# Where a split weight panel begins in its buffer: 256 bytes from its tokens in every product, in place of 0 or 32 bytes

## The reference, cut to what matters

```python
h = modulate(rms_norm(x_lat, g_attn[l]), sh1, sc1)
gl, mq, mk, mv, nq, nk, nv = mixer_proj(h, w_in, g_qa, w_uq, g_kva, w_ukv, ...)
y_mla = blocked_attention(mq, mk, mv)
y_na = neighborhood_attention(nq, nk, nv, nk_c, nv_c, rpb[l])
x_lat = x_lat + gt1 * gated_merge(gl, y_mla, y_na, w_mla_o[l], w_na_o[l], w_out[l])
...
h2 = modulate(rms_norm(x_lat, g_mlp[l]), sh2, sc2)
x_lat = x_lat + gt2 * jnp.square(jax.nn.relu(h2 @ w_ff1[l])) @ w_ff2[l]
```

## The kernel before, in words

| split matmuls | distance, stationary minus moving | how many |
|---|---|---|
| 512 columns | 0 | 4302 |
| 256 columns | -32 | 5028 |
| 256 columns (`first_features`, context part of k = 0) | 0 | 36 |
| 272 columns (`mv` panel 0) | -32, -96, -160, ... and so on in steps of 64 with k, eight values | 96 |

## Time and profile before

### The profile page before, as it was taken

How to read it: one execution, slowest core, us unless ns; L and a number is a source line. 1 busy time by engine, 2 the same in 40 slices (tenths; PEclk the granted TensorE clock), 3 DMA queues, 4 the chain that set the end, 5 groups by cost and what they waited for, 6 DMA issues and landing times. The chain is left out here.

```text
span 1984.6 us, 30374 instructions
## 1 busy us (share of the span) xinstructions
PE 1945.9 (98%) x12204; PEld 1635.7 (82%) x12204; DVE 1304.4 (66%) x2407; ACT 904.9 (46%) x1635; POOL 52.1 (3%) x78
## 2 busy tenths in 40 slices
PE   7999999999999999999999999999999999999998
PEld 5788778889888888898789899998887788888867
DVE  5447678857886665657665777675666464555886
ACT  4446763325423232456664654443444432234675
POOL 0000000001000000100000000000000000001000
PEclk9999999999999999999999999999999999999999
DMA  7322006543545454433139455554311133432411
GB/s 311 117 95 86 17 28 239 189 158 108 191 175 207 182 196 174 181 133 108 52 127 338 173 188 174 192 188 159 112 61 54 47 123 128 149 127 85 149 44 43
DMA packets 53579, 278.32 MB, mean 140 GB/s; under 512 B 4536, under 2 KB 19128, under 8 KB 24512
## 3 DMA queue, kind: packets, MB, share of 16 engines
q1 hardware_dynamic: 47168, 265.50, 37.2%
q10 hardware_dynamic: 6128, 10.03, 1.6%
q0 software_dynamic: 144, 0.85, 0.1%
HBM read 274.26 MB, written 2.11 MB: 139 GB/s over the span
## 5 line engine op out<-in xcount | busy, mean ns | idle before, releaser
L640 PE MATMUL ps<-t 128*128 128x512 f32 (+1 forms) x1936 | 665.7, 344 | 4.3 <-DVE t L2026 4.3
L641 PE MATMUL ps<-t 128*128 128x512 f32 (+1 forms) x1936 | 658.9, 340 | 0.0
L642 PE MATMUL ps<-t 128*128 128x512 f32 (+1 forms) x1936 | 658.7, 340 | 0.0
L2026 DVE TENSOR_TENSOR t<-t 128x1024 fp32r<-128x1024 f32 (+2 forms) x370 | 414.3, 1160 | 154.2 <-ACT t L1384 153.3
L1384 ACT ACTIVATE t<-t 128x1024 fp32r<-128x1024 f32 (+3 forms) x376 | 358.3, 1001 | 193.9 <-PE ps L642 142.1
L640 PEld LDWEIGHTS ps<-t 128*128 128x128 f32 x1936 | 363.6, 188 | 55.1 <-DVE t L2026 6.6
L642 PEld LDWEIGHTS ps<-t 128*128 128x128 f32 x1936 | 363.6, 188 | 42.5
L641 PEld LDWEIGHTS ps<-t 128*128 128x128 f32 x1936 | 363.7, 188 | 41.8 <-issue 0.7
L2012 DVE TENSOR_TENSOR t<-t 128x256 f32<-128x256 f32 (+9 forms) x622 | 227.1, 386 | 137.9 <-ACT t L1756 38.1
L2021 DVE SCALAR_TENSOR_TENSOR t<-t 128x256 f32<-128x256 f32 (+4 forms) x372 | 273.0, 766 | 36.4 <-ACT t L1489 21.8
L1489 ACT ACTIVATE t<-ps 128x512 f32<-128x512 f32 (+2 forms) x239 | 113.2, 494 | 284.6 <-PE ps L642 188.0
(11 more groups left out here) (191 smaller groups left out, 2314.0 us busy)
## 6 DMA issues: line engine op xcount, KB each, us to landing
t<-in_panels SPq DMA_DIRECT2D x231, 1024.0 KB, 4.9
t<-in_panels SPq DMA_DIRECT2D x12, 768.0 KB, 4.5
t<-in_panels SPq DMA_DIRECT2D x16, 512.0 KB, 3.6
t<-in_window ACTq DMA_DIRECT2D x4, 768.0 KB, 4.3
t<-gates_between ACTq DMA_DIRECT2D x4, 512.0 KB, 4.9
t<-in_panels SPq DMA_DIRECT2D x1, 1088.0 KB, 5.0
t<-in_ctxT SPq DMA_DIRECT2D x1, 1024.0 KB, 6.6
t<-in_xT SPq DMA_DIRECT2D x1, 1024.0 KB, 8.9
```

The lines of the kernel that those rows point to most:

```text
L640: e.matmul(o, hi[:, k, w], xh[:, c0:c1], start=k == 0, stop=False)
L641: e.matmul(o, hi[:, k, w], xl[:, c0:c1], start=False, stop=False)
L642: t = e.matmul(o, lo[:, k, w], xh[:, c0:c1], start=False, stop=k == p.nk - 1)
L2026: e.tensor_tensor(p.half(p.split(wlo), a), p.half(raw[p.slot], a), p.half(p.split(whi), a).bitcast(F32), ALU.subtract).then_inc(*up(ve, (" ...
```

## The change

`first_column` is replaced by a rule of two values. Nothing else changes: the instructions, their order, waits, sizes and DMAs are the same, and only the start addresses of panels within `whi` and `wlo` move.

```diff
 def first_column(key):
-    kind, l, n = key[0], key[1], key[-1]
-    if kind in ("uq", "mv") or kind == "na" and n >= 4:
-        return 8
-    if (kind == "ukv" or kind in ("mo", "no") and len(key) == 3 and l == 0 or kind == "wo" and l == 0 and n < 3
-            or kind == "ff2" and l == 0 and n < 15 or kind == "mw" and n < 7):
-        return 8
-    if kind in ("cq", "ckv", "gm", "gn", "ff1") and l == 1 or kind == "ff1" and n < 2 or kind == "mq" and n < 2 or kind == "atz":
-        return 120
-    return 0
+    kind = key[0]
+    return 72 if kind in ("ukv", "no", "wo", "ff2", "mw", "atw") or kind == "mo" and len(key) == 3 else 64
```

## The result

The changed kernel takes **1994.97 us** (median of 4 executions, 1994.24 to 1995.65), the kernel before 1985.93 in its 4 executions beside it: a ratio of 1.0044, 95% interval 1.0032 to 1.0056. The change costs 9 us. The profiled execution of the changed kernel took 1995.35 us, its span is 1993.2 against 1984.6.

A forecast was written before the change was run, and what follows sets the result against it. TensorE's start-to-start matmul pace was taken as the bound (busy 98% of the span). 512 columns 0, 256 columns +17.1 us, 2 us of waits given back: +15 us, forecast 2001 us, range 1942 to 2025.

The forecast's parts named there:

- the likeliest case: Whole kernel: 512-column matmuls unchanged, 256-column ones slower, 2001 us, its own range 1993 to 2009; chance 0.40.
- reading 3: Eight 256-column matmuls at distance 0, from 19.46 to 20.42 us: 120.0 ns start to start.
- the third rival: Place doesn't matter beyond +-32 near 0, the 3.4 ns belonged to the first 20 us: 1986 us; chance 0.17.
- The rival that 256 is quiet for both sizes: 512- and 256-column matmuls both lose disturbance at distance 256: 1924 us in full, 1955 by half; chance 0.33.
- the bounds: 512-column matmuls up to 34 us slower; undisturbed paces of 220 and 110 ns would gain 29 and 33 us.
- 0 and 256 are alike: Matmuls at distance 256 behave as at 0, since both agree by the remainder of 64: 512 columns stay at 226.7 ns.
- within 0.01 of 0.375: Three 272-column matmuls in the changed kernel were to take within 0.01 of 0.375 us.
- -32 and +32 are alike: Distances of either sign disturb matmuls equally, from the same 8 ns at 512-column panel changes.
- Reading 4: 512-column matmuls at +32 and -32, once each at a panel change: records of 397 and 396 ns against 389.
- 116.6 becomes 120.0, 3.4 ns x 5028: 256-column matmuls going from distance -32 to 256, each 3.4 ns slower: 17.1 us in all.
- Given back: I take half, 2 us: Line 640's waits for VectorE in layer 1, 4.2 us, shrink as TensorE slows: half, 2 us, given back.
- layer 1 longer by some 11 us: Layer 1's window from 830 to 1320 us lengthens by some 11 us, layer 0 and the mLSTM output unmoved.

The follow-up runs named there:

- e3_wide256: Kernel before with distance 256 for the 512-column products alone, the others as before: 1986.48 us against 1987.01, ratio 0.9998.
- e4_narrow256: Kernel before with distance 256 for the 256-column products alone, the others as before: 1995.85 us, ratio 1.0044.
- e7_wide32: Kernel before with distance 32 in place of 0 for the 512-column products, the others as before: 2009.52 us against 1987.55, ratio 1.0114.
- e1_sweep32: Kernel before with successive panels taking sixteen distances in turn, 0 to 480 bytes in steps of 32, counted apart for 512 and 256 columns: 2007.18 us.
- e6: Kernel before with distance 64 for the 256-column products, 0 for the 512-column ones: 1983.21 us against 1987.55, ratio 0.998.
- e8: Kernel before with distance 88 for the 256-column products, 0 for the 512-column ones: 1986.36 us against 1986.99, ratio 0.9999.
- e9: Kernel before with distance 76 for the 256-column products, 0 for the 512-column ones: 1986.9 us, ratio 1.0001.
- e11: Kernel before with 256-column products at 88 bytes where weights are stationary, 64 where tokens are, 512-column ones at 0: 1980.61 us against 1986.77, ratio 0.9971.
- e12: Kernel before with 256-column products at 64 bytes where weights are stationary, 88 where tokens are, 512-column ones at 0: 1986.06 us, ratio 0.9997.

## Why the prediction was right, and where its steps failed

**Direction and place: right.** 2001 was said, 1995 measured: slower, by 9 us instead of 15, within the likeliest case's own range. The losing matmuls are the 256-column ones at 120.0 ns start to start, the 512-column ones stayed at 227, and e3_wide256 and e4_narrow256 show the two halves separately. The 120 of reading 3 was no matter of the first 20 us, as the third rival had it: it holds in layer 1 from 926 us on. VectorE's and ScalarE's busy times are the same. The rival that 256 is quiet for both sizes is refuted: nothing fell. Nor did any of the 47 distances bring the 220 and 110 ns that the bounds took as free of disturbance; the lowest settled means are 226.7 and 113.3. The rule it was weighed against, that the Trainium skill ("TensorE: Matmul & The Clock Gate", part 2, step 1) gives the moving operand and the weight load independent read ports that do not slow each other, does not hold for these matmuls: e7_wide32 moves nothing but start addresses and costs 6.0 ns on each matmul of 512 columns.

**"0 and 256 are alike": right for the wrong reason.** The step that failed is "the coarse place in the 512 bytes counts little and the fine place, by 64, counts". It was drawn from the 272-column matmuls, eight distances with one remainder by 64 and one pace of 125. In e1_sweep32 the distances 0, 64, 128 and 192 give 226.7, 233.4, 232.8 and 228.9, so places that agree by 64 do not agree; those that agree by 256 do. The changed kernel's own 272-column rows show that the eight readings misled: at 0, -256 and +-128 they take 127.1 to 127.6 ns, at +-64 and +-192 124.7 to 125.2, where one value was expected for all. The mean, 125.8, hid it: "within 0.01 of 0.375" came true (3.02 / 8 = 0.378) and proved nothing. Had the change been to 64 or 192, the same reasoning would have said no change from 0 for 512 columns, and lost some 28 us (6.6 x 4302) or 9 (2.2 x 4302).

**"-32 and +32 are alike": roughly.** By 256, -32 is 224. For 512 columns 32 and 224 both give 233.3. For 256 columns they are 118.3 and 117.4, and before's own mean at -32 was 116.85, so even that differs with what stands around it. Reading 4 was thinner than it had to be: the trace of before has not two but thirteen such panel changes among the 512-column products, and each has a record of 396 or 397 ns.

**"116.6 becomes 120.0, 3.4 ns x 5028": 17.1 us said, 14.8 measured.** The rows read were settled ones of one stretch. Over all 256-column intervals without a wait it is 116.85 to 119.84, 3.0 ns, and some 100 of the 256-column intervals hold a wait in one of the two traces and do not count. The likeliest case's bracket has a slip: with the 2 us given back, 1993 to 2009 is 1.9 to 5.1 ns for each 256-column matmul, not 1.7 to 4.7; the 3.0 measured is in either.

**"Given back: I take half, 2 us": the term that was mis-sized.** Waits gave back 4.8 us in the trace (6.2 with the half-clock stretch) and 6 in e4_narrow256. The step looked at one line in one window. In the changed kernel that line's wait did fall by 2.1 us, as said:

```profile
PEld ps L633 <- DVE t L2019: 4.0, 7, 1.0
PE ps L633 <- DVE t L2019: 2.1, 4, 0.8
```

The rest is outside it. 3.3 of the 6.2 us lie in intervals that begin at matmuls other than those of 256 columns, and 1.4 of these are the clock: twelve of before's transposes on line 1056 took 213 ns start to start instead of 109, and they are the ones in the half-clock stretch from 941.3 us. The prediction's "granted in full in all 40 slices" passed over that stretch. The same doubled transposes stand in six of the experiments' profiled executions, at 942 to 958 us, each time with such a stretch. For these two reasons, the waits of other stages and the clock, "layer 1 longer by some 11 us" failed too: from 864 to 1326 us streaming grew by 8.2 and the rest fell by 5.2, which leaves 3.0.

**Waits give back what TensorE loses and take back what it gains.** All against the kernel before, in us (negative is faster). The first three columns are the profiled executions, whose sum is the difference of the spans within 0.3 (an interval between two starts counts as half-clock when it touches such a stretch in either trace and is not a streaming one); the last is the difference of the medians:

| kernel | streaming | half-clock stretches | waits and the rest | medians |
|---|---|---|---|---|
| the change | +14.8 | -1.4 | -4.8 | +9.0 |
| 256-column products at 256 (e4) | +14.9 | +0.2 | -6.2 | +8.8 |
| at 64 (e6) | -5.7 | -1.5 | +1.5 | -4.3 |
| at 88 (e8) | -4.6 | +1.8 | +3.5 | -0.6 |
| at 76 (e9) | -4.8 | -0.1 | +4.4 | -0.1 |
| 64 and 88 by role (e11) | -10.1 | +0.2 | +3.3 | -6.2 |
| 88 and 64 by role (e12) | -2.9 | +1.9 | +0.8 | -0.7 |
| 512-column products at 32 (e7) | +25.6 | +0.2 | -0.7 | +22.0 |

Of a gain in the 256-column rows waits take a quarter (e6) to nearly all (e9), of a loss they give back a third to two fifths; of the loss in the 512-column rows next to nothing.

The medians hold the clock too. The 71 executions of the kernel before that stand beside the experiments average 1985.2 us where 1.000 of the clock was granted (13 of them), 1987.0 at 0.999 (43) and 1988.7 at 0.998 (14). Against the 1985.2, the executions at 1.000 of the changed kernel average 1994.7 (3), of e7_wide32 2009.3 (3), of e6_narrow64 1981.1 (4) and of e11_mixed 1980.6 (4). So none of these four gains and losses is the clock's, but some 2 us of any one difference can be. e8_narrow88 had no execution at 1.000 among its eleven; at 0.999 it averages 0.2 us less than the kernel before (3 executions) and at 0.998 2.3 us less (6), so that a small gain of it is not ruled out.

## What to carry to other kernels

Two operands that are read at the same time can disturb each other by where they start, and a property read off a few neighbouring cases (here eight distances, all equal by 64) should be tried on a case that the rule would have to tell apart before it is built on. Sweep such a placement inside one program, but for every role that an operand can have: the best values of the sweep, 88 and 76, were best for one role only and gained nothing clear for the whole. And a change per instruction is not a change of the whole: from the sum take what the waits of all stages, not only of the stage in view, will give back or take. When two traces are subtracted, look at the granted clock of short windows first: one stretch of 3.4 us at half of it, which a slice of 50 us does not show, was worth 1.4 us here.

## What the runs showed of the hardware that was not expected

- An fp32r matmul whose stationary operand is replaced each time goes at a pace that depends on the distance between the moving operand and the next stationary one, by the remainder of 256 bytes, and between multiples of 32 also on which of the two the weights are: 226.7 to 235.0 ns for 512 columns, 113.3 to 121.5 for 256 (settled, both roles together). That it is the next load and not the own one is seen where the tokens change: own distance 0, next load 32 bytes off, and a record of 397 ns in place of 389. What repeats every 256 bytes no run here shows.
- The best place for one size is a bad one for the other: 0 gives the lowest interval at 512 columns and nearly the highest, 120.0, at 256.
- With stationary tokens the moving panel starts anywhere. Where its start is 8 bytes past a multiple of 16, eight of ten distances run at 119.9 to 121.0 ns; 4 bytes past, all six at 120.2 to 123.3; 12 bytes past, all five at 117.8 to 118.6; on a multiple, 114.2 to 119.5 but for the distances 0 and 160, which give 120.0. At 512 columns with stationary tokens, starts 4 bytes past take 233.3 to 240.0 ns and starts 12 bytes past 227.7 to 231.1, less than the starts on a multiple (231.1 to 236.9) but for the distances 0 (226.7) and 192 (229.1). With stationary weights, whose moving tokens always start on a multiple of 16, 88 gives 114.0 and 76 gives 113.4 at 256 columns. The Trainium skill ("SBUF — State Buffer", Specifications (TRN2)) says that SBUF has lines of 16 bytes and that each crossing to another line costs; the rows at 256 columns agree in sign for 4 and 8 bytes and not clearly for 12, those at 512 columns go the other way for 12, and no run separates this from the distance itself.
- At 64 bytes whole stretches of 256 columns run at 113.5 ns and others, with the same sizes and distance, at 117.8. What chooses between them is open. From these means, stationary weights at 76 and stationary tokens at 240 (113.4 and 114.8 ns) would be the next pair to try; it was not tried.
